# Softmax denominators of the second layer on ScalarE, and the low parts of its weights on GpSimd

## The chip, the cores and the metric

The kernel runs on one core of a Trainium2 chip, in one launch. The metric is the device time of that launch in microseconds (us). A core has TensorE (PE, matrix products; its weight loads are listed as PEld), VectorE (DVE), ScalarE (ACT), GpSimd (POOL) and SyncE (SP, which here issues all DMAs). Each engine takes its own instructions strictly in order; between engines there are only semaphores.

## The reference, cut to what matters

The program is one inference step of a two-layer encoder over 576 frames (512 of a prompt, 64 new ones with 256 cached). Layer 0 mixes with differential attention, layer 1 with forgetting attention (FoX); each is followed by a SwiGLU feed-forward part. The change lies in layer 1:

```python
def _fox_attend(q, k, v, cq, ck, q_pos, k_pos):
    s = jnp.einsum('bqhd,bkhd->bhqk', q, k) * (FOX_HEAD_DIM ** -0.5)
    s = s + cq^T[..., :, None] - ck^T[..., None, :]          # log-forget bias
    allowed = k_pos[None, :] <= q_pos[:, None]
    p = jax.nn.softmax(jnp.where(allowed, s, -jnp.inf), axis=-1)
    return jnp.einsum('bhqk,bkhd->bqhd', p.astype(v.dtype), v)
# 16 heads of 64; then  x += o @ w_o ;  x += swiglu(rmsnorm(x))
```

## The kernel before, in words

Activations lie transposed in SBUF, `xT` as 8 tiles of 128 features by 576 frames. Every weight comes as a stream of units of 128x1024 fp32, one unit for each 128 output columns. For precision each operand is split into a high and a low fp32r part: for a unit, ScalarE copies `w_raw` to `w_hi` (L908), and somebody subtracts `w_hi` from `w_raw` to give `w_lo`. TensorE adds the three products hi·hi, hi·lo and lo·hi (`slice_`, L570). There are two buffers of each, so unit u+1 is split while unit u is multiplied; the split of a unit must wait until the unit before the running one is used up (`w_used`).

`w_lo` is made by GpSimd (`lead`, L1262) in the feed-forward parts and in the output projections `wo`, and by VectorE (`weight_lo`, L1389) during both attention stages, where each unit has eight slots.

The attention of layer 1 is a schedule written out by hand. Time is cut into slots; a slot `t` holds one step of six matmuls of the projection (`project`). A group of two heads has 24 slots (three units: k, q, v). While group g+1 is projected, the attention of group g runs between the projection steps, and the last group runs between the steps of `wo`. The tables `F_...` name, for each small step and each engine, the slot `s` after the start of the group's attention in which it stands in that engine's queue. A slot orders an engine's own work; nothing else ties a step to a time.

For head h of group a the steps are: scores into `sps` (two banks; `score`, L635 to L643), row maximum on VectorE (L1462), exp on ScalarE (L1026), transposition on TensorE into `tps` (L658), its high part on ScalarE (`take_p`, L1048) and its low part on VectorE (`p_lo`, L1500), and the next transposition must wait for that low part, since `tps` is one buffer. Then come the products with V into `ops`: for the new frames (`pv_sample`, L694) and for the prompt (`pv_prompt`, L706). V is widened by ones, so the same product leaves the sum of each row, the softmax denominator, in the other 64 partitions of `ops`. VectorE takes its reciprocal into `rec` (L1516 for 64 new frames, L1526 for 512) and multiplies (L1518, L1528). The result is split for `wo` by ScalarE (`fox_o_hi`, L1065) and VectorE (`fox_o_lo`, L1534). `ops` and `tps` are free again only when `o_scaled` has been signalled by L1528; `transpose_v` of the next group (L671) and the next `pv_sample` wait for it.

Before the first group, GpSimd sets ones and zeros into the padded tiles of the layer and makes `f_lo`, the low part of the forget gate's weights (L1282), for which TensorE waits at L784.

Of the kernel before, what the change touches and what calls it, by code (L numbers as in the profile page):

```python
# [20 lines left out]
G = 8  # L21
# [19 lines left out]
WO_FOX_HI_AT, WO_FOX_SQ_AT = (50, 50, 52, 53, 53, 56, 58, 69), (52, 52, 52, 58, 60, 60, 62, 70)
WO_FOX_LO_AT, WO_FOX_SUM_AT = (51, 57, 57, 61, 62, 62, 64, 67), (50, 57, 57, 59, 62, 64, 67, 67)
WO_FOX_RES_AT = (7, 12, 19, 28, 35, 41, 47, 48, 50, 50, 52, 55, 58, 63)
WO_FOX_SPLIT_AT = (1, 10, 17, 24, 31, 45, 49, 55)
# [25 lines left out]
D_SPLIT = 1  # L70


F_SCORE, F_MAX, F_EXP = (2, 5, 5, 7, 7, 13, 13, 15, 18, 18), (1, 5, 5, 9, 10, 14, 14, 15, 18, 20), (1, 5, 6, 9, 9, 14, 14, 15, 18, 21)
F_TURN, F_TAKE_P, F_P_LO = (5, 7, 9, 11, 13, 15, 17, 18, 21, 24), (5, 7, 9, 11, 13, 15, 16, 18, 21, 23), (6, 7, 9, 11, 12, 15, 16, 18, 21, 22)
F_VT, F_TAKE_V, F_V_LO = (3, 2, 4)
F_PVS, F_TAKE_S, F_SUM_S = (7, 17), (8, 19), (9, 18)
F_PVP, F_SCALE_O, F_O_HI, F_O_LO = (15, 25), (15, 25), (16, 25), (17, 26)
F_K, F_Q, F_V = (8, 17, 24)
F_K_HI, F_K_LO, F_AUG = (11, 21), (13, 22), (17, 21)
F_Q_HI, F_Q_LO = (20, 21)  # L80
F_W_LO, F_SPLIT = (3, 1)
F_DUP_K, F_DUP_Q = (13, 23), 21
F_GATE_1, F_GATE_2, F_GATE_ACT = (9, 17, 13)
NORM0_AT = 3
NORM_AT = 2

# [52 lines left out]
def encoder(nc, w_units, w_forget, x_in, small, cst, cst16, rope_tab, k_past, v_past, f_past,  # L139
# [3 lines left out]
    with ExitStack() as ctx:  # L143
# [3 lines left out]
        def sem(name):  # L147
            return ctx.enter_context(nc.semaphore(name))
# [746 lines left out]
        def _(act):  # L895
# [244 lines left out]
            def fox_attention(t):  # L1140
                for a in range(G):
                    s, par, n = t - SLOTS * (a + 1), a % 2, Num(a)
                    for h in range(2):
                        if s == F_O_HI[h]:
                            fox_o_hi(a, h)
                    for tt in range(10):
                        if s == F_TAKE_P[tt]:
                            take_p(FOX, n, tt)
                    for jj in range(10):
                        if s == F_EXP[jj]:  # L1150
                            exps(FOX, n, par, jj)
# [102 lines left out]
        def _(pool):  # L1254
            def lead(u, kts=KT):

                u = u + 1
                slot = u.c % 2
                pool.wait_ge(w_hi_done, val(u + 1))
                if some(u - 1):  # L1260
                    pool.wait_ge(w_used, val(u - 1))
                nc.gpsimd.tensor_tensor(w_lo[slot][:, 0:kts, :], w_raw[slot][:, 0:kts, :],  # L1262
                                        w_hi[slot][:, 0:kts, :].bitcast(F32), ALU.subtract).then_inc(w_lo_done, 1)
# [5 lines left out]

            def fox_layer():  # L1270

                pool.wait_ge(w_used, U_LAYER)
                pool.wait_ge(acc_done, 3 * KT)
                for tile, value in ((vh2[:, :, 1:3, :], 1.0), (vl2[:, :, 1:3, :], 0.0)):
                    nc.gpsimd.memset(tile.bitcast(F32), value).then_inc(fox_set, 2)
                pool.wait_ge(fox_set, 4)
                nc.gpsimd.memset(kb[64:128, 0, :].bitcast(F32), 1.0).then_inc(fox_set, 1)
                pool.wait_ge(fox_set, 5)
                nc.gpsimd.memset(kb[0:64, 1, :].bitcast(F32), 1.0).then_inc(fox_set, 1)
                pool.wait_ge(fox_set, 6)  # L1280
                pool.wait_ge(f_hi_done, 1)
                nc.gpsimd.tensor_tensor(f_lo[:], f_raw[:], f_hi[:].bitcast(F32), ALU.subtract).then_inc(f_lo_done, 1)  # L1282
                nc.gpsimd.memset(kf[:, T:TQ], 0.0).then_inc(fox_set, 1)
                nc.gpsimd.memset(vf[:, T:TQ], 0.0).then_inc(fox_set, 1)
                for q in range(2):
                    nc.gpsimd.memset(qa[q][:, :, T:TQ].bitcast(F32), 0.0)
                    op = nc.gpsimd.memset(qb[q][:, :, T:TQ].bitcast(F32), 0.0)
                op.then_inc(fox_set, 1)
                for m in range(KT):
                    lead(Num(U_LAYER + U_WO + m))  # L1290

            pool.wait_ge(w_hi_done, 1)
            nc.gpsimd.tensor_tensor(w_lo[0][:, KT // 2:KT, :], w_raw[0][:, KT // 2:KT, :],
# [42 lines left out]
        def _(dve):  # L1336
# [165 lines left out]
            def o_sum(L, a, h):  # L1502

                dve.wait_ge(os_taken, val(v_index(L, a, h) + 1))
                if L == DIFF and later(a):
                    dve.wait_ge(ol_done, val(a))
                tt(og[:, SEQ:T] if L == DIFF else osum[:], os2[:, 0:NEW], os2[:, NEW:2 * NEW], ALU.add
                   ).then_inc(os_summed, 1)

            def scale_sample(a, h):  # L1510

                r, o, i = slice(64 * h, 64 * h + 64), slice(64 - 64 * h, 128 - 64 * h), 2 * a + h
                dve.wait_ge(os_summed, G + i + 1)
                if a > 0:
                    dve.wait_ge(op_lo, i - 1)
                nc.vector.reciprocal(rec[r, SEQ:T], osum[o, :]).then_inc(rec_done, 1)  # L1516
                dve.wait_ge(rec_done, 2 * i + 1)
                tt(rec[r, SEQ:T], osum[r, :], rec[r, SEQ:T], ALU.mult).then_inc(os_scaled, 1)  # L1518

            def scale_prompt(a, h):  # L1520

                r, o, i = slice(64 * h, 64 * h + 64), slice(64 - 64 * h, 128 - 64 * h), 2 * a + h
                dve.wait_ge(pvp_done, G + i + 1)
                if a > 0:
                    dve.wait_ge(op_lo, i - 1)
                nc.vector.reciprocal(rec[r, 0:SEQ], ops[o, :]).then_inc(rec_done, 1)  # L1526
                dve.wait_ge(rec_done, 2 * i + 2)
                tt(rec[r, 0:SEQ], ops[r, :], rec[r, 0:SEQ], ALU.mult).then_inc(o_scaled, 1)  # L1528

            def fox_o_lo(a, h):  # L1530

# [78 lines left out]
            def fox_attention(t):  # L1610
                for a in range(G):
                    s, par, n = t - SLOTS * (a + 1), a % 2, Num(a)
                    for h in range(2):
                        if s == F_SCALE_O[h]:
                            scale_prompt(a, h)
                        if s == F_O_LO[h]:
                            fox_o_lo(a, h)
                    for jj in range(10):
                        if s == F_MAX[jj]:
                            row_max(FOX, n, par, jj)  # L1620
                    if s == F_V_LO:
                        v_lo(FOX, n)
                    for tt_ in range(10):
                        if s == F_P_LO[tt_]:
                            p_lo(FOX, n, tt_)
                    for h in range(2):
                        if s == F_SUM_S[h]:
                            o_sum(FOX, n, h)
                            scale_sample(a, h)

            def fox_layer():
                dve.wait_ge(r_ready, 3)
                for t in range(SLOTS * G + WO_ALL):
# [242 lines left out]
```

## Time and profile before

| | us |
|---|---|
| median of 3 runs (1566.44 to 1574.3) | 1572.11 |
| the profiled execution, its own time | 1574.79 |
| its span, first to last instruction | 1572.8 |
| attention stage of layer 1, about | 790 to 1107 |

The profile shows busy time by engine, a timeline in 40 slices, the chain of work that ended last, groups of instructions by line, and for any stretch what each engine did, what it waited for and at what clock TensorE ran. A busy TensorE is not one at its peak: after idle stretches its granted clock can be at the lower of two levels.

### The profile page before, as it was taken

What the parts mean: (1) busy time and instruction counts of PE and PEld (TensorE: products, weight loads), DVE (VectorE), ACT (ScalarE), POOL (GpSimd) and SP (SyncE); (2) the same over time, 40 slices, a digit from 0 to 9 for tenths busy, and PEclk for the clock granted to TensorE, in tenths of its full rate; (3) what the DMA queues carried; (4) which work ended last, traced back from release to release, by engine and by line L of the source; (5) the groups of instructions that cost most, each with busy time, mean ns of one, the idle gap of its engine ahead of it and who ended that gap; (6) DMA issues with size and microseconds to landing.
All of it is one profiled execution on the core that took longest, in us unless ns stands there. A gap on an engine that the chain in (4) does not pass through costs nothing.

```text
span 1572.8 us, 28185 instructions
## 1 busy us (share of the span) xinstructions
PE 1492.7 (95%) x10911; PEld 1446.0 (92%) x10911; DVE 665.7 (42%) x1073; ACT 587.1 (37%) x988; POOL 433.9 (28%) x216
## 2 busy tenths in 40 slices
PE   6999999999999999998888888988999999999996
PEld 6899999999999999998888888888999999999996
DVE  6787786611111111221577777776611111111212
ACT  4566665432222222222344444443432222222121
POOL 2000002244444444334000000002344444443331
PEclk9999999999999999999999999989999999999998
DMA  5433332222222222223322222221222222222222
GB/s 170 126 99 109 102 99 81 67 81 80 80 81 84 88 80 75 84 87 104 88 73 79 80 82 82 82 71 49 68 81 83 88 82 80 80 80 85 84 78 83
DMA packets 47592, 135.04 MB, mean 86 GB/s; under 512 B 6480, under 2 KB 11088, under 8 KB 47520
## 3 DMA queue, kind: packets, MB, share of 16 engines
q1 hardware_dynamic: 47520, 134.06, 27.7%
q8 instruction: 48, 0.79, 0.2%
q14 instruction: 24, 0.20, 0.0%
HBM read 111.22 MB, written 11.83 MB: 78 GB/s over the span
## 4 chain that ended last, share of the span: by engine, by line
PE 87%; DVE 7%; issue 2%; ACT 2%; POOL 1%; DMA 0%; SPq 0%; DVEq 0%; ACTq 0%; POOLq 0%
PE ps L570 74%; DVE rec L1526 3%; PE ops L706 3%; PE tps L658 2%; PE sps L617 2%; PE ops L694 1%; PE sps L635 1%; PE sps L641 1%; DVE rec L1528 1%; PE tps L671 1%; PE sps L620 1%; PE sps L784 1%; PE ops L713 0%; DVE w_lo L1389 0%; PE sps L590 0%
## 5 line engine op out<-in xcount | busy, mean ns | idle before, releaser
L1262 POOL TENSOR_TENSOR w_lo<-w_raw,w_hi 128x1024 fp32r<-128x1024 f32 (+1 forms) x153 | 359.7, 2351 | 1108.5 <-ACT w_hi L908 1108.5
L570 PE MATMUL ps<-xh,w_hi 128*128 128x288 f32 x2176 | 487.0, 306 | 18.3 <-DVE xl L1729 11.5
L570 PE MATMUL ps<-xl,w_hi 128*128 128x288 f32 x2176 | 471.5, 299 | 0.0
L570 PE MATMUL ps<-xh,w_lo 128*128 128x288 f32 x2176 | 470.9, 298 | 0.0
L908 ACT ACTIVATE w_hi<-w_raw 128x1024 fp32r<-128x1024 f32 (+1 forms) x200 | 208.2, 1041 | 451.0 <-PE ps L570 448.4
L570 PEld LDWEIGHTS ps<-xh,w_hi 128*128 128x128 f32 x2176 | 354.2, 193 | 21.4 <-issue 20.1
L570 PEld LDWEIGHTS ps<-xl,w_hi 128*128 128x128 f32 x2176 | 356.3, 192 | 0.0
L570 PEld LDWEIGHTS ps<-xh,w_lo 128*128 128x128 f32 x2176 | 355.4, 191 | 0.0
L570 PE MATMUL ps<-hh,w_lo 128*128 128x288 f32 x704 | 150.8, 294 | 0.0
L570 PE MATMUL ps<-hh,w_hi 128*128 128x288 f32 x704 | 149.8, 294 | 0.0
L570 PE MATMUL ps<-hl,w_hi 128*128 128x288 f32 x704 | 149.5, 293 | 0.0
L1377 DVE TENSOR_TENSOR uf<-ps,rs 128x576 f32<-128x576 f32 x44 | 33.3, 757 | 231.7 <-PE ps L570 231.7
L1766 DVE TENSOR_TENSOR hl<-hf,hh 128x576 f32 (+1 forms) x44 | 33.4, 759 | 228.5 <-ACT hh L1229 228.5
L1371 DVE TENSOR_TENSOR xT<-ps,xT 128x576 f32<-128x576 f32 (+1 forms) x44 | 33.2, 755 | 224.0 <-PE ps L570 223.6
L570 PEld LDWEIGHTS ps<-hh,w_hi 128*128 128x128 f32 x704 | 113.3, 187 | 0.0
L570 PEld LDWEIGHTS ps<-hl,w_hi 128*128 128x128 f32 x704 | 112.5, 188 | 0.0
L570 PEld LDWEIGHTS ps<-hh,w_lo 128*128 128x128 f32 x704 | 112.4, 188 | 0.0
L1229 ACT ACTIVATE hh<-hf 128x576 f32 (+1 forms) x44 | 30.1, 685 | 178.3 <-POOL hf L1316 178.3
L1462 DVE TENSOR_REDUCE nmax<-sps 128x1 f32<-128x384 f32 (+3 forms) x160 | 74.8, 496 | 29.0 <-PE sps L620 20.4
L1500 DVE TENSOR_TENSOR ptl<-tps,pth 128x512 fp32r<-128x512 f32 (+1 forms) x96 | 46.8, 488 | 77.1 <-ACT pth L1048 77.0
L658 PE MATMUL tps<-cstf,pr 128*128 128x128 f32 x312 | 57.0, 285 | 20.9 <-DVE pts L1500 20.7
L1026 ACT ACTIVATE pr<-sps,nmax 128x384 f32<-128x384 f32 (+3 forms) x80 | 42.2, 538 | 59.1 <-DVE nmax L1462 58.6
(182 smaller groups left out, 1739.7 us busy)
## 6 DMA issues: line engine op xcount, KB each, us to landing
w_raw<-w_units SPq DMA_DIRECT2D x184, 512.0 KB, 3.5
w_raw<-w_units SPq DMA_DIRECT2D x16, 384.0 KB, 3.0
qsw<-qsin SPq DMA_DIRECT2D x64, 72.0 KB, 2.0
ka<-ka SPq DMA_DIRECT2D x16, 224.0 KB, 3.0
xT<-x_in SPq DMA_DIRECT2D x8, 288.0 KB, 5.5
dk_out<-kf SPq DMA_DIRECT2D x8, 288.0 KB, 2.5
dv_out<-vf SPq DMA_DIRECT2D x8, 288.0 KB, 2.2
fk_out<-kf SPq DMA_DIRECT2D x8, 288.0 KB, 2.2
```

Of the source, the lines that this page charges most:

```text
L570: mm = nc.tensor.matmul(out[:, half, :], w[:, k, :], rhs[:, kt, half * HALF:(half + 1) * HALF], start=start and w is w_hi[slot] and rhs is ...
L658: mm = nc.tensor.transpose(tps[:, b, :], pr[:, slot, P * b:P * b + P], ident)
L706: mm = nc.tensor.matmul(ops[:, P * j:SEQ], w, p[:, j, P * j:SEQ], start=j == 0 and v is hi and p is pth, stop=j == 3 and v is lo)
L908: nc.scalar.activation(w_hi[slot][:, 0:kts, :], w_raw[slot][:, 0:kts, :], ACT.Copy).then_inc(w_hi_done, 1)
L1026: nc.scalar.activation(pr[:, slot, 0:width(i)], sps[:, jj % 2, 0:width(i)], ACT.Exp, bias=nmax[:, slot:slot + 1]).then_inc(exp_done, 1)
L1262: nc.gpsimd.tensor_tensor(w_lo[slot][:, 0:kts, :], w_raw[slot][:, 0:kts, :], w_hi[slot][:, 0:kts, :].bitcast(F32), ALU.subtract).then_inc( ...
L1371: tt(halves(at(xT, k)), proj(n.c % 2), halves(at(xT, k)), ALU.add).then_inc(ps_read, 1)
L1377: tt(halves(dst), proj(n.c % 2), halves(scale), ALU.mult).then_inc(ps_read, 1)
L1462: nc.vector.tensor_reduce(nmax[:, slot:slot + 1], sps[:, jj % 2, 0:width(i)], AX_X, ALU.max, negate=True).then_inc(max_done, 1)
L1500: tt(dst, src, hi.bitcast(F32), ALU.subtract).then_inc(pt_lo, 1)
L1526: nc.vector.reciprocal(rec[r, 0:SEQ], ops[o, :]).then_inc(rec_done, 1)
L1766: tt(at(hl, jt), hf[:], at(hh, jt).bitcast(F32), ALU.subtract).then_inc(hl_done, 1)
```

## The change

- The two reciprocals of a head leave VectorE. ScalarE takes the logarithm of the new frames' denominators (`log_sample`, 64 columns) and of the prompt's (`recip`, 512 columns from `ops`), then one exp with factor -1 over all 576 columns. VectorE keeps the two multiplications (`scale_o`), now behind a wait for ScalarE.
- In layer 1's attention stage, `w_lo` of 23 units is made by GpSimd (`lead`) instead of VectorE (`weight_lo`).
- GpSimd makes `f_lo` first in the layer, ahead of its memsets.
- The slots of the layer's tables are shifted: `transpose_v` from 3 to 4, the first score from 2 to 3, the multiplication of head 0 from 15 to 16, high part of the output of head 0 from 16 to 17, and smaller ones.

```diff
-F_PVP, F_SCALE_O, F_O_HI, F_O_LO = (15, 25), (15, 25), (16, 25), (17, 26)
+F_PVP, F_SCALE_O, F_O_HI, F_O_LO = (15, 25), (16, 25), (17, 25), (17, 28)
+F_LN_S, F_RECIP = (10, 21), (15, 25)
-F_SCORE, ... = (2, 5, 5, 7, 7, 13, 13, 15, 18, 18), ...
+F_SCORE, ... = (3, 4, 5, 7, 7, 13, 13, 15, 18, 18), ...
-F_VT, F_TAKE_V, F_V_LO = (3, 2, 4)
+F_VT, F_TAKE_V, F_V_LO = (4, 1, 4)
@@ ScalarE
+            def log_sample(a, h):
+                r, o, i = slice(64 * h, 64 * h + 64), slice(64 - 64 * h, 128 - 64 * h), 2 * a + h
+                act.wait_ge(os_summed, G + i + 1)
+                if a > 0:
+                    act.wait_ge(op_lo, i - 1)
+                nc.scalar.activation(rec[r, SEQ:T], osum[o, :], ACT.Ln).then_inc(den_logs, 1)
+            def recip(a, h):
+                r, o, i = slice(64 * h, 64 * h + 64), slice(64 - 64 * h, 128 - 64 * h), 2 * a + h
+                act.wait_ge(pvp_done, G + i + 1)
+                nc.scalar.activation(rec[r, 0:SEQ], ops[o, :], ACT.Ln).then_inc(den_logs, 1)
+                act.wait_ge(den_logs, 2 * i + 2)
+                nc.scalar.activation(rec[r, :], rec[r, :], ACT.Exp, scale=-1.0).then_inc(rec_done, 1)
@@ GpSimd, fox_layer
+                pool.wait_ge(f_hi_done, 1)
+                nc.gpsimd.tensor_tensor(f_lo[:], f_raw[:], f_hi[:].bitcast(F32), ALU.subtract).then_inc(f_lo_done, 1)
                 pool.wait_ge(w_used, U_LAYER)
                 pool.wait_ge(acc_done, 3 * KT)
...
-                pool.wait_ge(f_hi_done, 1)
-                nc.gpsimd.tensor_tensor(f_lo[:], f_raw[:], f_hi[:].bitcast(F32), ALU.subtract).then_inc(f_lo_done, 1)
...
-                for m in range(KT):
-                    lead(Num(U_LAYER + U_WO + m))
+                for m in range(1, U_IN):
+                    lead(Num(U_LAYER + m))
@@ VectorE
-            def scale_sample(a, h):
...
-                nc.vector.reciprocal(rec[r, SEQ:T], osum[o, :]).then_inc(rec_done, 1)
...
-            def scale_prompt(a, h):
...
-                nc.vector.reciprocal(rec[r, 0:SEQ], ops[o, :]).then_inc(rec_done, 1)
...
+            def scale_o(a, h):
+                r, i = slice(64 * h, 64 * h + 64), 2 * a + h
+                dve.wait_ge(rec_done, i + 1)
+                tt(rec[r, 0:SEQ], ops[r, :], rec[r, 0:SEQ], ALU.mult).then_inc(o_scaled, 1)
                 tt(rec[r, SEQ:T], osum[r, :], rec[r, SEQ:T], ALU.mult).then_inc(os_scaled, 1)
@@ VectorE, fox_layer
-                    if t % KT == F_W_LO and KT <= t < SLOTS * G:
-                        weight_lo(U_LAYER + t // KT + 1)
```

## Rows read from the trace of the kernel before

**Rows 1.** The page: busy times, and the granted clock in 40 slices
```profile
PE 1492.7 (95%) x10911; PEld 1446.0 (92%) x10911; DVE 665.7 (42%) x1073; ACT 587.1 (37%) x988; POOL 433.9 (28%) x216
...
PEclk9999999999999999999999999989999999999998
```
**Rows 2.** Chain that ended last, 850 to 1180: by line, then start, us, what
```profile
by line: PE ps L570 43.7%; DVE rec L1526 13.3%; PE ops L706 7.9%; PE tps L658 4.9%; issue 4.3%; PE ops L694 3.1%; PE sps L635 2.8%; DVE rec L1528 2.7%; PE sps L641 2.5%; PE tps L671 1.8%; DVE nmax L1462 1.3%; DVE w_lo L1389 1.2%; ACT ka L97
...
954.48 1.58 PE ps L570 x12
```
**Rows 3.** Windows: stretch, length, busy us by engine, then PEclk, DMA share, GB/s
```profile
790.00:831.00 41.00, 36.21 (x246) 33.81 (x245) 30.84 (x46) 19.62 (x37) 0.00 (x0) 0.92 0.26 81
912.90:953.80 40.90, 35.59 (x243) 33.33 (x242) 30.61 (x46) 19.29 (x36) 0.00 (x0) 0.92 0.27 78
1070.00:1107.00 37.00, 33.38 (x239) 31.73 (x237) 21.47 (x33) 13.23 (x26) 7.38 (x3) 0.95 0.13 44
100.00:140.00 40.00, 40.00 (x300) 36.31 (x298) 31.42 (x72) 26.33 (x64) 0.00 (x0) 1.00 0.34 101
```
**Rows 4.** Timeline of TensorE, one group: idle time before, and its releaser
```profile
935.82 0.50 PE L706 MATMUL ops<-pth,vh 128*128 128x512 f32 x1 [0.57 <-DVE ptl L1500]
942.21 1.09 PE L671 MATMUL tps<-cstf,vf 128*128 128x128 f32 x4 [2.15 <-DVE rec L1528]
965.62 0.69 PE L658 MATMUL tps<-cstf,pr 128*128 128x128 f32 x4 [2.59 <-DVE pts L1500]
```
**Rows 5.** Timeline of VectorE in the same group
```profile
937.99 3.35 DVE L1526 RECIPROCAL rec<-ops 64x512 f32<-64x512 f32 x1 [0.31 <-PE ops L706]
941.37 0.69 DVE L1528 TENSOR_TENSOR rec<-ops,rec 64x512 f32<-64x512 f32 x1
...
964.67 0.54 DVE L1462 TENSOR_REDUCE nmax<-sps 128x1 f32<-128x384 f32 x1
965.14 0.34 DVE L1500 TENSOR_TENSOR pts<-tps,pts 128x192 fp32r<-128x192 f32 x1
```
**Rows 6.** Windows behind four idle times of TensorE, columns as in rows 3
```profile
745.40:751.40 6.00, 5.92 (x22) 5.36 (x23) 0.00 (x0) 0.75 (x2) 0.68 (x6) 0.53 0.01 3
775.30:779.30 4.00, 2.23 (x13) 1.79 (x13) 2.88 (x4) 3.57 (x5) 0.00 (x0) 1.00 0.62 122
...
942.20:946.20 4.00, 3.99 (x19) 3.91 (x19) 3.56 (x6) 2.29 (x5) 0.00 (x0) 0.58 0.04 9
...
1065.80:1069.80 4.00, 3.94 (x30) 3.55 (x31) 3.44 (x7) 2.45 (x7) 0.00 (x0) 1.00 0.01 4
```
**Rows 7.** ScalarE: groups of the whole span (busy, mean ns), then one window
```profile
L1079 ACT ACTIVATE ors<-ops,eps 128x512 f32<-128x512 f32 x8 | 5.5, 687 | 3.1 <-PE tps L714 3.1
L1083 ACT ACTIVATE ors<-ors 128x576 f32<-128x576 f32 x8 | 5.5, 686 | 0.3
...
L1225 ACT ACT_TABLE_LOAD x2 | 2.6, 1283 | 0.0
...
965.60:976.70 11.10, 10.52 (x70) 10.21 (x70) 7.56 (x15) 8.46 (x16) 0.00 (x0) 0.85 0.23 53
```
**Rows 8.** `w_lo` by VectorE; then GpSimd and VectorE at 718; L1348 over all
```profile
L1389 DVE TENSOR_TENSOR w_lo<-w_raw,w_hi x46: 1204/1216/1228, 31.0 to 1054.9; 128x1024 fp32r<-128x1024 f32 x46
...
718.21 2.40 POOL L1262 TENSOR_TENSOR w_lo<-w_raw,w_hi 128x1024 fp32r<-128x1024 f32 x1 [2.36 <-ACT w_hi L908]
...
718.97 2.26 DVE L1348 SCALAR_TENSOR_TENSOR xl<-xT,smalls,xh  x1 [1.08 <-ACT xh L922]
...
L1348 DVE SCALAR_TENSOR_TENSOR xl<-xT,smalls,xh x24: 805/814/2275, 297.5 to 1138.0; 128x576 fp32r<-128x576 f32 x16, - x8
```
**Rows 9.** Timelines of ScalarE, GpSimd and TensorE where the second layer begins
```profile
737.98 1.06 ACT L1160 ACTIVATE f_hi<-f_raw 128x1024 fp32r<-128x1024 f32 x1 [1.16 <-DMA f_raw<-w_forget]
...
742.99 2.34 POOL L1282 TENSOR_TENSOR f_lo<-f_raw,f_hi 128x1024 fp32r<-128x1024 f32 x1
...
745.48 0.82 PE L784 MATMUL sps<-xh,f_hi 128*128 128x288 f32 x2 [4.81 <-POOL f_lo L1282]
```

More of the change, by code:

```diff
@@ L40 @@
 WO_END = [max(q for q, s in enumerate(WO_STEPS) if s[0] == j) for j in range(WO_RUNS)]
[L41 to L44, printed above, removed]
+WO_FOX_HI_AT, WO_FOX_SQ_AT = (50, 50, 53, 53, 53, 55, 58, 69), (52, 52, 52, 57, 60, 60, 62, 70)
+WO_FOX_LO_AT, WO_FOX_SUM_AT = (51, 57, 57, 61, 62, 62, 64, 67), (50, 57, 57, 58, 62, 64, 67, 69)
+WO_FOX_RES_AT = (7, 12, 19, 29, 35, 47, 47, 48, 50, 50, 52, 57, 58, 63)
+WO_FOX_SPLIT_AT = (1, 12, 18, 24, 31, 45, 48, 55)
 WO_HI_AT, WO_SQ_AT = (49, 50, 51, 53, 53, 56, 58, 69), (50, 50, 54, 57, 60, 61, 61, 71)
@@ L70 @@
 D_SPLIT = 1
-F_SCORE, F_MAX, F_EXP = (2, 5, 5, 7, 7, 13, 13, 15, 18, 18), (1, 5, 5, 9, 10, 14, 14, 15, 18, 20), (1, 5, 6, 9, 9, 14, 14, 15, 18, 21)
+F_SCORE, F_MAX, F_EXP = (3, 4, 5, 7, 7, 13, 13, 15, 18, 18), (1, 5, 5, 9, 9, 12, 14, 15, 18, 18), (1, 5, 6, 9, 9, 14, 15, 15, 18, 19)
 F_TURN, F_TAKE_P, F_P_LO = (5, 7, 9, 11, 13, 15, 17, 18, 21, 24), (5, 7, 9, 11, 13, 15, 16, 18, 21, 23), (6, 7, 9, 11, 12, 15, 16, 18, 21, 22)
-F_VT, F_TAKE_V, F_V_LO = (3, 2, 4)
-F_PVS, F_TAKE_S, F_SUM_S = (7, 17), (8, 19), (9, 18)
-F_PVP, F_SCALE_O, F_O_HI, F_O_LO = (15, 25), (15, 25), (16, 25), (17, 26)
-F_K, F_Q, F_V = (8, 17, 24)
-F_K_HI, F_K_LO, F_AUG = (11, 21), (13, 22), (17, 21)
+F_VT, F_TAKE_V, F_V_LO = (4, 1, 4)
+F_PVS, F_TAKE_S, F_SUM_S = (7, 17), (8, 19), (7, 19)
+F_PVP, F_SCALE_O, F_O_HI, F_O_LO = (15, 25), (16, 25), (17, 25), (17, 28)
+F_LN_S, F_RECIP = (10, 21), (15, 25)
+F_K, F_Q, F_V = (9, 17, 24)
+F_K_HI, F_K_LO, F_AUG = (11, 21), (14, 22), (17, 21)
 F_Q_HI, F_Q_LO = (20, 21)
-F_W_LO, F_SPLIT = (3, 1)
-F_DUP_K, F_DUP_Q = (13, 23), 21
-F_GATE_1, F_GATE_2, F_GATE_ACT = (9, 17, 13)
+_, F_SPLIT = (3, 1)
+F_DUP_K, F_DUP_Q = (15, 23), 21
+F_GATE_1, F_GATE_2, F_GATE_ACT = (9, 19, 13)
 NORM0_AT = 3
@@ L352, in encoder @@
         fox_set = sem("fox_set")
+        den_logs = sem("den_logs")
         rec_done = sem("rec_done")
@@ L1143, in fox_attention @@
                     for h in range(2):
+                        if s == F_RECIP[h]:
+                            recip(a, h)
                         if s == F_O_HI[h]:
@@ L1156, in fox_attention @@
                             take_o_sample(FOX, n, h)
+                        if s == F_LN_S[h]:
+                            log_sample(a, h)
             def fox_layer():
@@ L1506, in o_sum @@
                     dve.wait_ge(ol_done, val(a))
+                if L == FOX and some(a * 2 + h):
+                    dve.wait_ge(os_scaled, val(a * 2 + h))
                 tt(og[:, SEQ:T] if L == DIFF else osum[:], os2[:, 0:NEW], os2[:, NEW:2 * NEW], ALU.add
                    ).then_inc(os_summed, 1)
-            def scale_sample(a, h):
[L1512 to L1515, printed above, removed]
-                nc.vector.reciprocal(rec[r, SEQ:T], osum[o, :]).then_inc(rec_done, 1)
-                dve.wait_ge(rec_done, 2 * i + 1)
-                tt(rec[r, SEQ:T], osum[r, :], rec[r, SEQ:T], ALU.mult).then_inc(os_scaled, 1)
-            def scale_prompt(a, h):
[L1522 to L1525, printed above, removed]
-                nc.vector.reciprocal(rec[r, 0:SEQ], ops[o, :]).then_inc(rec_done, 1)
-                dve.wait_ge(rec_done, 2 * i + 2)
-                tt(rec[r, 0:SEQ], ops[r, :], rec[r, 0:SEQ], ALU.mult).then_inc(o_scaled, 1)
+            def scale_o(a, h):
+                r, i = slice(64 * h, 64 * h + 64), 2 * a + h
+                dve.wait_ge(rec_done, i + 1)
+                tt(rec[r, 0:SEQ], ops[r, :], rec[r, 0:SEQ], ALU.mult).then_inc(o_scaled, 1)
+                tt(rec[r, SEQ:T], osum[r, :], rec[r, SEQ:T], ALU.mult).then_inc(os_scaled, 1)
             def fox_o_lo(a, h):
@@ L1614, in fox_attention @@
                         if s == F_SCALE_O[h]:
-                            scale_prompt(a, h)
+                            scale_o(a, h)
                         if s == F_O_LO[h]:
@@ L1628, in fox_attention @@
                             o_sum(FOX, n, h)
-                            scale_sample(a, h)
             def fox_layer():
```

## The prediction

> **What bounds the kernel now.** First the page: TensorE is busy for 95% of the span, at nearly its full clock but for one slice of 40 that shows an 8 [rows 1]. So most of the time belongs to TensorE and this change can't touch it. Then the chain of work that ended last, cut to the attention stage of the second layer: there the 512-column reciprocal L1526 alone holds 13.3% and its multiplication 2.7% [rows 2]. VectorE is on the path there, in front of TensorE.
>
> Then the stage group by group. One group of two heads takes 41 us, in which TensorE is busy for 36.2 in the first and 35.6 in a later one, at a granted clock of 0.92; the same stage of the first layer, which has no 512-column reciprocal, shows TensorE busy for 40.00 of 40 us at clock 1.00 [rows 3]. Between the two group rows shown lie two more groups, and behind them two, that read the same within 0.1 us. So a group loses two things: some 5.3 us of idle TensorE, and 0.08 × 41 = 3.3 us of speed.
>
> The timeline of TensorE names the idle times of one group: 2.15 us ahead of `transpose_v`, which waits for L1528; 2.59 us ahead of the transposition of head 1, which waits for `p_lo`; and 0.57 us ahead of the second `pv_prompt` [rows 4]. On VectorE the first is the reciprocal (3.35) and its multiplication (0.69) in a row, which `transpose_v` waits out; the second is the same pair for head 0, with a row maximum and the small `p_lo` queued behind it, done at 965.48, 0.14 us before TensorE starts [rows 5]. The clock: after the 2.15 us idle time the next 4 us are granted 0.58, between the two levels of 2.4 and 1.2 GHz; after 4.81 us, 0.53 over 6 us. After an equal 2.15 us at 1065.8 it stayed at 1.00, and so it did around the idle times of 775 to 779, 1.77 us in all [rows 6]. Short idle times keep the clock; long ones mostly lose it.
>
> **The change part by part.** *Reciprocals.* Out go 3.35 us and one of 64 columns for each head on VectorE; in come a logarithm of 512 columns, one of 64 and an exp of 576 on ScalarE. The first layer has a logarithm of 512 columns out of `ops` at 687 ns and an exp of 576 at 686 ns [rows 7]; the new ones have 64 partitions instead of 128, and I take the same time. So from the end of `pv_prompt` to `o_scaled`: 0.69 + 0.69 + 0.69 for the multiplication [rows 5] and some 0.2 for hand-overs, 2.3 us, against the 4.22 us that it takes now from 937.99 to 942.21 [rows 4, 5]. That alone brings 2.15 down to 0.25 us, and `transpose_v` stands one slot later, which is another 0.79 us of projection (12 matmuls, two slots, take 1.58 us [rows 2]). This idle time goes. At the second, `p_lo` no longer stands behind the reciprocal in VectorE's queue: it stands ahead of `scale_o`. But on ScalarE `take_p` now stands behind `recip`: ready 0.81 us after `pv_prompt`, it starts at about 1.4 us, and the exp of the next score follows it. I count 1.4 + 0.35 for `take_p`, 0.6 for that exp and 0.1 for the hand-over: 2.45 us, while TensorE has its own work until about 2.3 us. 2.59 us becomes 0.1 to 0.2. What is late next is the `pv_sample` of head 1, which waits for `scale_o`, at 2.9 us: 0.2 us more.
>
> *`w_lo` to GpSimd.* VectorE loses 23 instructions of 1.216 us, 28 us in all; GpSimd takes 2.40 us for one [rows 8]. A unit has eight slots, over 8 × 0.79 = 6.3 us, and TensorE needs `w_lo` only at the unit's first step, so the 1.2 us more lie under that. SP's next load waits for `w_lo` too, but stands five slots behind the split. The cover goes only if GpSimd starts over 2 us later than I assume. Per group VectorE falls from 30.6 us by 6.7 + 1.1 + 3.7 to about 19; ScalarE rises from 19.3 to 22.6 [rows 3, 5, 8]; GpSimd has 7.2. In a group of 32 to 34 us none is a bound by its sum.
>
> *What the move costs.* GpSimd's `w_lo` gets in VectorE's way. At 718.97 an `xl` of VectorE that normally takes 0.81 us took 2.26, begun while a `w_lo` of GpSimd ran from 718.21 to 720.61: it ended at 721.23, 0.6 us behind it [rows 8]. In the new queue ScalarE's split of a unit at slot 17 stands just ahead of head 0's `fox_o_hi` (0.68 us), so the `fox_o_lo` behind it meets a GpSimd instruction that has run for 0.6 us and waits out the other 1.8. Behind it on VectorE stand the row maxima of the last two scores and a `p_lo`; the exps, and TensorE's transposition of slot 21, wait for them. TensorE has 0.4 us of slack there; I count 1.0 us of idle time. The next stretch, up to the second `pv_prompt`, is full on ScalarE: 8.46 of 11.1 us busy, where TensorE by itself would need 11.1 - 0.6 - 0.15 × 11.1 = 8.9 [rows 7]. So the 0.57 us ahead of `pv_prompt` stays. Sum of new and remaining idle time: 0.1 + 0.2 + 1.0 + 0.6, some 2.0 us for each of seven groups (the eighth runs beside `wo` and has no such split). Bounds: 0, if the queues have more slack than I count, and 4, if every hand-over is late; I take 2.0, as the row at 718.97 is the same pair of engines.
>
> The Trainium skill (SBUF — State Buffer, "Who interferes with whom") says that a VectorE instruction with two inputs in SBUF and a GpSimd instruction that reads SBUF exclude each other, and that whichever begins second is blocked until the first ends. The row at 718.97 agrees. By that rule the sum is the one here; without it 1.5 us in each of seven groups, about 10 us, would come off.
>
> *Clock.* Idle times of 1 us or less should keep it at 1.00, as the 1.77 us around 775 do [rows 6]. Then the 3.3 us of each group come back.
>
> *`f_lo` first.* `f_hi` is done at 739.04, GpSimd starts `f_lo` at 742.99, and TensorE has waited 4.81 us when it starts at 745.48 [rows 9]. Made at once, `f_lo` is done at 741.4: 3.9 us sooner. The idle time left is about 0.9 us, so I count the 6 us at 0.53 back as well, 2.8 us [rows 6]. The memsets now end later, but are wanted only some 8 us on. The other shifted slots cost nothing that I can find: they order work that waits for TensorE anyway; if one does cost, it lies within the 0 to 4 us.
>
> **The sum.** Idle time to win: six groups from 790 to 1035.6 with 4.8 + 5 × 5.3 = 31.3, a seventh like them 4.8, the last stretch 3.6: 39.7. Speed: 7 × 3.3 + 0.05 × 37 = 25. Together 64.7 [rows 3]. Less 7 × 2.0 = 14: 50.7. With 3.9 + 2.8 at the start: 57.4. From the profiled execution's 1574.79 that gives 1517.4. The median shown is 2.7 us lower than that execution: 1515.
>
> **The rivals.**
> (a) *The new idle times don't appear.* For it speaks that in the first layer VectorE at 31.4 of 40 and ScalarE at 26.3 hold TensorE up nowhere [rows 3]; against it the row at 718.97. The 14 come back: 1501.
> (b) *The clock doesn't recover.* The remaining idle times cluster or grow to 2 us, and TensorE goes on losing speed behind them as it does now. For it speaks that ScalarE's stretch up to the second `pv_prompt` is nearly full and strictly in order [rows 7]; against it the idle times of 775. Then the 25 and the 2.8 stay lost: 1543.
> (c) *Logarithm and exp need different tables.* A table load takes 1283 ns [rows 7]; with two of them for each head the chain is 2.3 + 2.6 = 4.9 us, longer than 4.22, and `transpose_v` gains nothing: only `f_lo` remains, about 1566. That would be a change that doesn't do what it says. Against it: the first layer takes both functions in turn eight times, and the span's loads lie elsewhere [rows 7].
> The skill (ScalarE: Activation LUTs, "Table sets: the hidden batching unit") names one set that holds both; the trace agrees.
> (d) *Slower.* GpSimd's `w_lo` meets VectorE on TensorE's path three times in a group, for each unit and not only at slot 17. If each time TensorE stands for the 2.4 us and loses about 1.7 us of speed behind it (4 us at 0.58), a group pays 12.3 us and wins back 8.6: 3.7 × 7 = 26 more, less 6.7 at the start, 1591. It decides from 8.6 us of new idle time and lost speed in a group. Against it: at the other two splits VectorE mostly has instructions whose source is PSUM queued.
>
> **How the numbers follow.** Forecast 1515: 0.57, in its own bounds of 0 to 4 us a group 1501 to 1529. (a) 0.17, (b) 0.18, (c) 0.04, (d) 0.04. The range takes in (a) and (b): 1499 to 1544, and leaves out (c), (d) and the far ends. About 0.5%, 8 us, is what a measurement of this kernel can tell from no change: faster by more 0.93, within it 0.03, slower by more 0.04.
>
> **What would show it.** In the new profile: TensorE busy for all but about 2 us of a group, a group of 33 to 35 us, clock 0.98 or more between 790 and its end; no idle time over 0.5 us ahead of `transpose_v`; `fox_o_lo` of head 0 at over 2 us instead of 0.75, and an idle time of about 1 us behind it; the wait at L784 under 1.5 us. Wrong it is if `transpose_v` still waits, if the clock stays at 0.92, or if TensorE waits for GpSimd's `w_lo`.

## The result

| | median, us | ratio to before, 95% interval |
|---|---|---|
| before | 1572.41 (1566.44 to 1574.3, 4 runs) | |
| after | 1517.74 (1516.01 to 1519.7, 4 runs) | 0.9659 (0.963 to 0.9688) |

The forecast was 1515, in a range of 1499 to 1544. The profiled execution of after took 1518.45 us, with a span of 1516.7.

The page of after, its line of busy times and of the granted clock, against [rows 1]:

```profile
PE 1467.4 (97%) x10911; PEld 1422.0 (94%) x10911; DVE 588.8 (39%) x1018; ACT 609.9 (40%) x1036; POOL 491.5 (32%) x239
...
PEclk9999999999999999999999999999999999999998
```

VectorE is busy for 77 us less, ScalarE for 23 and GpSimd for 58 us more. Two slices of 40 showed an 8 before, the 27th and the last; the 27th, which lies in the stage, is back at 9. Now TensorE in one group of after; the columns are start, us, engine, line, operation, and the idle time before it with its releaser:

```profile
837.07 0.41 PE L660 MATMUL tps<-cstf,pr 128*128 128x128 f32 x2 [0.94 <-ACT pr L1028]
841.45 0.51 PE L708 MATMUL ops<-pth,vh 128*128 128x512 f32 x1 [0.68 <-DVE ptl L1522]
```

These are the only idle times of the group, and the same two stand in all seven, 34.1 us apart. Those of 2.15 and 2.59 us [rows 4] are gone; what remains is the 0.57 us ahead of the second `pv_prompt`, now 0.68, and a new one of 0.94 us. In place of the reciprocal stand a logarithm and an exp on ScalarE, then the multiplication on VectorE (ns of one, min/median/max, first and last start in us):

```profile
L1071 ACT ACTIVATE rec<-ops x16: 589/592/595, 794.2 to 1046.4; 64x512 f32<-64x512 f32 x16
L1073 ACT ACTIVATE rec<-rec x16: 681/686/687, 794.8 to 1047.0; 64x576 f32<-64x576 f32 x16
L1538 DVE TENSOR_TENSOR rec<-ops,rec x16: 670/683/695, 796.2 to 1047.7; 64x512 f32<-64x512 f32 x16
```

Two windows of after answer to [rows 3] and [rows 6] (stretch, length, busy us of PE, PEld, DVE, ACT and POOL, PEclk, DMA share, GB/s):

```profile
815.70:849.80 34.10, 32.48 (x243) 30.27 (x242) 20.96 (x39) 22.09 (x43) 7.47 (x3) 1.00 0.33 94
773.00:777.00 4.00, 1.92 (x7) 1.48 (x8) 3.13 (x4) 1.78 (x4) 2.16 (x1) 0.77 0.89 221
```

A group is 34.1 us long instead of 40.9, TensorE is idle in it for 1.6 us instead of 5.3, and its clock is 1.00 instead of 0.92. The second window is the one bad spot of the new stage: its beginning. There VectorE and GpSimd of after read:

```profile
763.20 0.61 DVE L1690 TENSOR_SCALAR ncum<-cumh 32x896 f32<-32x896 f32 x1 [1.02 <-ACT cumh L1214]
763.84 1.08 DVE L1693 TENSOR_TENSOR ncum<-cumh,cum 32x896 f32<-32x896 f32 x1
764.95 2.71 DVE L1690 TENSOR_SCALAR ncum<-cumh 32x896 f32<-32x896 f32 x1
```
```profile
764.18 2.99 POOL L1284 TENSOR_TENSOR w_lo<-w_raw,w_hi 128x1024 fp32r<-128x1024 f32 x1 [14.48 <-ACT w_hi L910]
```

The same instruction takes 0.61 us alone and 2.71 beside GpSimd's `w_lo`, which runs until 767.17. It negates the cumulative forget sums, on the chain to the first score, and so TensorE waits longer there:

```profile
741.84 0.51 PE L786 MATMUL sps<-xh,f_hi 128*128 128x288 f32 x2 [0.96 <-POOL f_lo L1295]
...
773.83 0.42 PE L637 MATMUL sps<-ka,qa 128*128 128x384 f32 x1 [3.92 <-issue]
775.50 0.69 PE L643 MATMUL sps<-kb,qb 128*128 128x384 f32 x1 [1.25 <-DMA qb<-qa]
```

The first row is the wait for `f_lo`, 0.96 us instead of 4.81 [rows 9]. The second and third are the first score: 5.2 us of idle time. (What the profile calls "issue" ends 0.1 us after VectorE's `fox_q_lo`, for which that score waits.)

Three marks in TensorE's timeline split the difference: the end of the layer's first unit (the start at L786 less its idle time), the first product of the first `pv_prompt`, and the first product of the last block of the last one. The distances between them, in us, read in the same way from one profiled execution of each kernel below:

| | first unit to first `pv_prompt` | from there to the last | from there to the end of the span |
|---|---|---|---|
| before | 54.7 | 304.7 | 472.7 |
| after | 51.3 | 253.7 | 470.8 |
| only the reciprocals moved | 47.7 | 247.0 | 471.1 |
| only `w_lo` moved | 59.7 | 304.8 | 472.4 |
| only `f_lo` first | 48.3 | 305.4 | 472.7 |
| after, `fox_o_hi` of head 0 at 16 | 51.9 | 256.6 | 470.5 |
| after, late `aug_left` and `fox_q_lo` | 52.3 | 262.1 | 470.9 |
| after, early split | 47.7 | 253.9 | 471.2 |
| these three together | 49.0 | 264.9 | 472.2 |
| after, memsets for `w_lo` | 49.4 | 242.9 | 470.5 |
| after, `fox_o_hi` and `fox_o_lo` at 16 | 52.0 | 241.9 | 471.5 |
| the same with the early split | 50.4 | 241.8 | 471.1 |
| only the reciprocals moved, old slots | 50.1 | 251.2 | 471.5 |

So after gains 3.4 us at the start, 51.0 in the attention stage and 1.9 behind it. The first column is the least sure: kernels with the same instructions at the start of the layer differ in it by up to 2.7 us, by the clock that the execution got there: the early split alone reads 47.7 and together with both `fox_o` edits 50.4, with 5.1 us of idle time each, but with a granted clock of 1.00 over 775 to 779 in the one and 0.50 over 771.5 to 775.5, the like place, in the other.

### The profile page after: what moved, and what is told of

It reads as the page before. It is cut to its first block, busy times and chain, and to the rows that moved or that the text cites. A ratio compares the mean times of both kernels' runs of the same rounds, so it can differ in the third digit from the quotient of the medians.

```text
span 1516.7 us, 28200 instructions
## 1 busy us (share of the span) xinstructions
PE 1467.4 (97%) x10911; PEld 1422.0 (94%) x10911; DVE 588.8 (39%) x1018; ACT 609.9 (40%) x1036; POOL 491.5 (32%) x239
## 4 chain that ended last, share of the span: by engine, by line
PE 90%; ACT 3%; DVE 3%; issue 2%; DMA 1%; POOL 0%; SPq 0%; DVEq 0%; ACTq 0%
PE ps L572 78%; PE ops L708 3%; PE tps L660 2%; PE sps L619 2%; PE sps L637 1%; PE sps L643 1%; PE ops L696 1%; ACT w_hi L910 1%; DVE ol L1545 1%; PE sps L622 1%; PE tps L673 0%; PE ops L715 0%; DMA xT<-x_in 0%; PE sps L786 0%; ACT ka L976 0%
## 5 line engine op out<-in xcount | busy, mean ns | idle before, releaser
L1284 POOL TENSOR_TENSOR w_lo<-w_raw,w_hi 128x1024 fp32r<-128x1024 f32 (+1 forms) x176 | 417.3, 2371 | 995.6 <-ACT w_hi L910 995.6
L572 PE MATMUL ps<-xh,w_hi 128*128 128x288 f32 x2176 | 481.6, 303 | 16.4 <-ACT xh L1223 8.7
L572 PEld LDWEIGHTS ps<-xh,w_hi 128*128 128x128 f32 x2176 | 349.6, 190 | 19.4 <-issue 17.9
L572 PEld LDWEIGHTS ps<-xh,w_lo 128*128 128x128 f32 x2176 | 351.8, 189 | 0.0
L572 PEld LDWEIGHTS ps<-xl,w_hi 128*128 128x128 f32 x2176 | 351.8, 189 | 0.0
L1393 DVE TENSOR_TENSOR xT<-ps,xT 128x576 f32<-128x576 f32 (+1 forms) x44 | 33.2, 755 | 224.6 <-PE ps L572 224.3
L1338 POOL TENSOR_TENSOR hf<-sg,uf 128x576 f32<-128x576 f32 x44 | 62.8, 1427 | 0.0
```

The lines of the kernel that those rows point to most:

```text
L572: mm = nc.tensor.matmul(out[:, half, :], w[:, k, :], rhs[:, kt, half * HALF:(half + 1) * HALF], start=start and w is w_hi[slot] and rhs is ...
L1338: nc.gpsimd.tensor_tensor(hf[:], sg[:], uf[:], ALU.mult).then_inc(hf_done, 1)
L1393: tt(halves(at(xT, k)), proj(n.c % 2), halves(at(xT, k)), ALU.add).then_inc(ps_read, 1)
```

## The experiments

My theory behind them: TensorE was held up by VectorE's queue behind the reciprocal, and the idle time cost its length and the clock after it; the move of `w_lo` brings nothing of that and costs, because GpSimd shuts VectorE out. The rival: VectorE was simply too full, and both loads had to leave it.

**Only the reciprocals moved.** In the changed kernel, back to `w_lo` on VectorE:

```diff
 # VectorE, fox_layer
+                    if t % KT == F_W_LO and KT <= t < SLOTS * G:     # F_W_LO = 3
+                        weight_lo(U_LAYER + t // KT + 1)
 # GpSimd, fox_layer
-                for m in range(1, U_IN):
-                    lead(Num(U_LAYER + m))
+                for m in range(KT):
+                    lead(Num(U_LAYER + U_WO + m))
```

> The changed kernel, with w_lo of the attention stage's 23 units made by VectorE again (at slots 3, 11 and 19, as before the change). My theory (VectorE's queue behind the reciprocal held TensorE up; the move of w_lo is no part of the gain and costs the 0.94 us idle time behind fox_o_lo in each of 7 groups): 1518 us +-8, no fox_o_lo over 1 us, group between 33 and 35 us, but a new idle time of about 1 us where v_lo stands behind w_lo on VectorE. Rival (VectorE's total load was the bound, so that both reciprocals and w_lo have to leave it): a group over 36 us, 1535 or more.

Measured: 1505.71 us, ratio 0.9593 (0.9575 to 0.9612): faster than after, the intervals don't overlap, and it lies below the 1518 ± 8 that I expected. Here is one of its groups, then what remains of idle time in it:

```profile
810.20:843.40 33.20, 32.59 (x243) 30.42 (x242) 22.76 (x41) 22.12 (x42) 0.00 (x0) 1.00 0.33 97
```
```profile
865.93 0.50 PE L708 MATMUL ops<-pth,vh 128*128 128x512 f32 x1 [0.28 <-DVE ptl L1522]
873.68 0.55 PE L660 MATMUL tps<-cstf,pr 128*128 128x128 f32 x3 [0.34 <-DVE vl L1512]
```

The idle time behind `v_lo` is there, at 0.34 us a third of what I expected. VectorE with 22.8 of 33.2 us busy holds TensorE up for no more than these 0.6 us. The rival falls: the reciprocals, with `f_lo` and the new slots, are more than the whole gain, and moving `w_lo` costs 10 to 12 us of it (10 by the two ratios, 12 by the two medians).

**Only `w_lo` moved.** In the kernel before:

```diff
-                    if t % KT == F_W_LO and KT <= t < SLOTS * G:
-                        weight_lo(U_LAYER + t // KT + 1)
 # GpSimd, fox_layer
-                for m in range(KT):
-                    lead(Num(U_LAYER + U_WO + m))
+                for m in range(1, U_IN):
+                    lead(Num(U_LAYER + m))
```

> The kernel before, with only w_lo of the attention stage moved to GpSimd; reciprocals, slots and f_lo as before. My theory: both idle times of 2.1 and 2.6 us behind the reciprocals stay, a group takes 40 to 41.5 us, 1572 +-6 us. Rival (VectorE's total load was the bound): half of the gain or more, 1550 or less.

Measured: 1577.17 us, ratio 1.0048 (1.0029 to 1.0067): a small loss. The groups are as long as before (304.8 us to the last `pv_prompt`, 304.7 before), and both idle times of TensorE stand as they did [rows 4]:

```profile
864.61 0.63 PE L671 MATMUL tps<-cstf,vf 128*128 128x128 f32 x4 [2.15 <-DVE rec L1528]
887.16 1.09 PE L658 MATMUL tps<-cstf,pr 128*128 128x128 f32 x4 [2.59 <-DVE pts L1500]
```
```profile
846.39:887.16 40.77, 35.75 (x242) 33.33 (x242) 30.56 (x42) 19.26 (x37) 7.44 (x3) 0.92 0.27 79
849.41 2.69 DVE L1534 TENSOR_TENSOR ol<-rec,oh 64x576 fp32r<-64x576 f32 x1
```

But VectorE is not freer: it loses 3.7 us of `w_lo` in a group, and reads busy for 30.56 us in the window, as before [rows 3]. GpSimd shuts out `fox_o_lo` here too, 2.69 us instead of 0.75, and `osum`, 1.56 instead of 0.22, in 7 groups. So the run shows that this move by itself shortens neither idle time; what a VectorE really freed of 3.7 us would do, it doesn't show. The loss lies at the start of the layer, 59.7 against 54.7 us. There `ncum` takes 2.70 us, as in after.

**Only `f_lo` first.** In the kernel before, the two lines of `f_lo` ahead of `pool.wait_ge(w_used, U_LAYER)`:

> The kernel before, with only f_lo moved ahead of GpSimd's memsets. My theory: the wait at L784 falls from 4.8 to about 1 us and the clock behind it stays at 1.00, and nothing later in the start of the layer takes that back: 6 us less, 1566. Rival (the chain from the forget gate to the first score takes it back): 2 us less or nothing, 1570 to 1572.

Measured: 1565.99 us, ratio 0.9973 (0.9961 to 0.9986), 4.2 us less (2.2 to 6.1). The wait at L784 is 1.05 us, and the first `pv_prompt` comes 6.4 us sooner after the first unit (48.3 instead of 54.7); the next stretch is 0.7 us longer in the profile. The size at that place is as forecast, what comes out at the end of it is a little less.

**GpSimd writing but not reading.** In the changed kernel, for the 23 units of the attention stage:

```diff
-                lead(Num(U_LAYER + m))         # tensor_tensor w_lo <- w_raw, w_hi
+                nc.gpsimd.memset(w_lo[u % 2][:].bitcast(F32), 0.0).then_inc(zeroed, 1)
+                pool.wait_ge(zeroed, m)
+                nc.gpsimd.memset(w_lo[u % 2][:].bitcast(F32), 0.0).then_inc(w_lo_done, 1)
```

> The changed kernel, with GpSimd's subtraction for w_lo of the attention stage's 23 units replaced by two memsets of the same tile one after the other, so that GpSimd writes and doesn't read; it leaves out the low part of those weights. My theory (reading is what shuts out a VectorE instruction with two inputs in SBUF): fox_o_lo of head 0 takes 0.75 us although GpSimd runs beside it, the idle time behind it goes, about 1511. Rival (any GpSimd instruction shuts VectorE out): fox_o_lo still lasts until GpSimd's memset ends, over 1.2 us.

Measured: 1503.29 us in one run. VectorE's `fox_o_lo` in it, and GpSimd beside it:

```profile
860.38 0.75 DVE L1554 TENSOR_TENSOR ol<-rec,oh 64x576 fp32r<-64x576 f32 x1 [0.16 <-ACT oh L1084]
```
```profile
859.84 0.95 POOL L1317 MEMSET w_lo<- 128x1024 f32 x1 [10.53 <-ACT w_hi L911]
860.85 0.96 POOL L1319 MEMSET w_lo<- 128x1024 f32 x1
```

GpSimd runs, and `fox_o_lo` takes its 0.75 us, beginning 0.54 us into a memset. In after it reads

```profile
833.45 2.48 DVE L1545 TENSOR_TENSOR ol<-rec,oh 64x576 fp32r<-64x576 f32 x1 [0.16 <-ACT oh L1083]
```
```profile
832.93 2.39 POOL L1284 TENSOR_TENSOR w_lo<-w_raw,w_hi 128x1024 fp32r<-128x1024 f32 x1 [10.09 <-ACT w_hi L910]
```

and ends at 835.93, 0.6 us after GpSimd. So for this instruction it is GpSimd's reading that shuts VectorE out. The Trainium skill (SBUF — State Buffer, "Who interferes with whom") says just this of a VectorE instruction with two inputs in SBUF, and that a GpSimd instruction that only writes does not exclude it; both rows agree. The time lies 8 us below the 1511 expected: the 0.94 us are gone in all groups, the 0.68 us ahead of `pv_prompt` are down to 0.26, and `ncum` at the start of the layer keeps its time.

**Who begins first.** Two kernels on one question: can order alone save `fox_o_lo`? In the changed kernel:

```diff
 # first
-F_O_HI, F_O_LO = (17, 25), (17, 28)
+F_O_HI, F_O_LO = (16, 25), (17, 28)
 # second
-F_O_HI, F_O_LO = (17, 25), (17, 28)
+F_O_HI, F_O_LO = (16, 25), (16, 28)
```

> The changed kernel, with fox_o_hi of head 0 at slot 16 instead of 17, so that it stands on ScalarE ahead of the split of a weight unit, and fox_o_lo on VectorE begins before GpSimd's w_lo. My theory (VectorE's fox_o_lo is shut out while GpSimd reads): fox_o_lo 0.75 instead of 2.47 us, the 0.94 us idle time behind it goes in 7 groups, 6 us less than the changed kernel: 1511. Rival (the idle time comes from ScalarE's order and not from fox_o_lo's length): 1517 to 1518, the idle time at slot 21 stays.

Measured: 1519.47 us, ratio 0.9682 (0.9666 to 0.9698): no gain. `fox_o_hi` stands ahead of the split now, but the eviction of q stands ahead of `fox_o_lo` on VectorE:

```profile
830.60 0.75 DVE L1399 TENSOR_TENSOR qf<-ps,rs 128x576 f32<-128x576 f32 x1
831.26 2.74 DVE L1545 TENSOR_TENSOR ol<-rec,oh 64x576 fp32r<-64x576 f32 x1
```
```profile
830.99 2.41 POOL L1284 TENSOR_TENSOR w_lo<-w_raw,w_hi 128x1024 fp32r<-128x1024 f32 x1 [10.48 <-ACT w_hi L910]
```

GpSimd begins 0.27 us before it, and the idle time behind is longer (1.33 us). My edit had not done what I meant it to do. The second does:

> The changed kernel, with both fox_o_hi and fox_o_lo of head 0 at slot 16, so that fox_o_lo stands on VectorE ahead of the q projection's eviction too and begins before GpSimd's w_lo does. My theory (of fox_o_lo and w_lo the one that begins second waits, and with only fox_o_hi moved fox_o_lo still began 0.27 us too late): fox_o_lo at 0.75 us in all 8 groups, no idle time at slot 21, GpSimd's w_lo later instead without anyone waiting for it; 6 us less than the changed kernel, about 1511. Rival (the idle time at slot 21 has another cause in the order of the queues): it stays near 1 us, 1517 to 1520.

Measured: 1505.38 us, ratio 0.9582 (0.9562 to 0.9602), 12 us less than after. A window as long as one group, which is now 32.4 us, and VectorE against GpSimd:

```profile
797.80:830.20 32.40, 32.40 (x243) 30.39 (x242) 19.31 (x39) 22.12 (x43) 7.48 (x4) 1.00 0.35 99
```
```profile
828.71 0.75 DVE L1545 TENSOR_TENSOR ol<-rec,oh 64x576 fp32r<-64x576 f32 x1 [0.75 <-ACT oh L1083]
```
```profile
830.19 2.40 POOL L1284 TENSOR_TENSOR w_lo<-w_raw,w_hi 128x1024 fp32r<-128x1024 f32 x1 [10.48 <-ACT w_hi L910]
```

TensorE is busy without a break, and `fox_o_lo` is over before GpSimd begins. The gain is twice what I had expected for this run: I had counted the 0.94 us alone, but the 0.67 us ahead of the second `pv_prompt` goes with it. The two were for the most part one delay, handed on through ScalarE's queue. In after, the row maximum stands behind `fox_o_lo`, and the exp behind the row maximum:

```profile
835.86 0.60 DVE L1484 TENSOR_REDUCE nmax<-sps 128x1 f32<-128x256 f32 x2
```
```profile
836.30 0.73 ACT L1028 ACTIVATE pr<-sps,nmax 128x256 f32<-128x256 f32 x2 [1.57 <-DVE nmax L1484]
```

From there ScalarE works without a listed break up to the copy (`take_p`) for which VectorE's last `p_lo`, and so the second `pv_prompt`, waits. With the memsets, where `fox_o_lo` is short at its old slot, 0.26 of the 0.68 us stays; that part goes only with the new order.

**The idle time ahead of `pv_prompt`, by later steps.**

```diff
-F_AUG = (17, 21)         # aug_left, ScalarE
+F_AUG = (17, 23)
-                        if s == F_Q_LO:                       # 21
+                        if s == (F_Q_LO if g else 21):        # 23
```

> The changed kernel, with aug_left of head 1 (0.78 us on ScalarE) and fox_q_lo (1.52 us on VectorE, group 0 left as it was) moved behind the last transposition's take_p and p_lo, from slot 21 to 23. My theory (the 0.67 us ahead of the second pv_prompt is ScalarE's and VectorE's queue ahead of that last p_lo): the idle time falls under 0.2 us in 7 groups, 4 us less than the changed kernel, 1514. Rival (it is the plain latency of transposition, copy and subtraction): it stays at 0.5 us or more, 1517 to 1518.

Measured: 1525.46 us, ratio 0.9706 (0.9688 to 0.9724): 8 us more than after. The idle time there does fall below what a listing shows, but `fox_q_lo` has moved into the next `w_lo`:

```profile
877.67 3.62 DVE L1475 SCALAR_TENSOR_TENSOR qa<-qf,qa 64x576 fp32r<-64x576 f32 x2
```
```profile
878.02 2.65 POOL L1284 TENSOR_TENSOR w_lo<-w_raw,w_hi 128x1024 fp32r<-128x1024 f32 x1 [6.92 <-ACT w_hi L910]
```

Two instructions of 0.76 us take 3.62; the multiplication behind them starts 2 us late, and TensorE stands for 1.06 us ahead of the first score of the next group. The same mechanism again, in a place that I had not looked at.

**The early split.** ScalarE splits the layer's fourth unit before it waits for the cumulative sums, so that `w_lo` is over before `ncum`:

```diff
 # ScalarE, forget
+                lead(Num(U_LAYER + 2))
                 act.wait_ge(f_step, 8)
                 nc.scalar.activation(cumh[:], cum[:], ACT.Copy).then_inc(cum_hi, 1)
```

(and the slot loop leaves that unit out).

> The changed kernel, with ScalarE's split of the fourth weight unit of the layer moved ahead of its wait for the cumulative sums, so that GpSimd's w_lo of that unit is over before VectorE negates the sums (ncum). My theory (that ncum instruction took 2.71 instead of 0.61 us because GpSimd was reading and writing beside it, and it lies on the chain to the first score): ncum back to 0.61 us, first score 2 us sooner, clock behind it better kept: 3 us less than the changed kernel, 1515. Rival (the chain to the first score is bounded elsewhere, by the copies by DMA): 1517 to 1518.

Measured: 1515.3 us, ratio 0.9643 (0.9626 to 0.9661). From the first unit to the first `pv_prompt` it is 47.7 us instead of 51.3; the wait of the first score falls from 3.92 to 2.06 us, and `ncum` is short again:

```profile
765.02 0.62 DVE L1691 TENSOR_SCALAR ncum<-cumh 32x896 f32<-32x896 f32 x1
```
```profile
771.82 0.41 PE L637 MATMUL sps<-ka,qa 128*128 128x384 f32 x1 [2.06 <-issue]
```

The place is right: with the early split (or the memsets) the first column of the table reads 47.7 to 50.4 us, in the kernels of after without it 51.3 to 52.4. The 2.4 us of the whole time are near the 3 expected, though its two intervals overlap.

**Together.** The first edit of `fox_o_hi`, the late steps and the early split:

> The edits of the three runs with fox_o_hi at slot 16, the late aug_left and fox_q_lo, and the early split, together in the changed kernel. My theory (they are separate idle times of TensorE): the sum of the three, 13 us less, 1505, and a group of 32.5 us without idle time over 0.3 us. Rival (each idle time taken out shows up in the next wait): 1511 or more.

Measured: 1526.11 us, ratio 0.9714 (0.9694 to 0.9734). Of the three only the early split helped by itself, and the sum shows it: 49.0 us at the start, 264.9 in the attention stage. The run was planned as a sum of gains of which two were none.

Then the edit that puts both `fox_o_hi` and `fox_o_lo` at slot 16, with the early split and without the late steps:

> The same edit together with the early split of the fourth weight unit. My theory: the two idle times are separate, 6 + 3 us less than the changed kernel, about 1508; that is still not below the kernel in which only the reciprocals moved (1505.7), since the idle time ahead of the second pv_prompt remains. Rival (w_lo on GpSimd can be made free by order alone): 1505 or less.

Measured: 1502.66 us, ratio 0.9576 (0.9557 to 0.9594): both edits that work, in the changed kernel. It is the fastest of the full kernels tried here, below before and after; from the kernel with only the reciprocals moved it can't be told apart. It lies 2.7 us below the `fox_o_lo` edit alone, the size that the early split had by itself, but these two intervals overlap as well. I had expected 1508, with the 0.67 us ahead of `pv_prompt` still in it.

**The slots.** The kernel with only the reciprocals moved, with the layer's tables `F_SCORE` to `F_GATE` as they were before the change (those of `wo` stay as in after):

> The kernel in which only the reciprocals moved (w_lo on VectorE, f_lo first), but with the slots of the layer as they were before the change, the multiplication of head 0 at slot 15 again. My theory (the reciprocals are the gain, the slots trim it): about 0.3 us ahead of transpose_v, and 1.0 us ahead of the transposition of head 1, because the small p_lo stands behind the multiplication and its wait for ScalarE; 1515. Rival (without new slots the waits stay long): 1.5 us or more at both places with a clock of 0.95 or less, 1530 or more.

Measured: 1512.44 us, ratio 0.9629 (0.961 to 0.9648). A group takes 33.7 us (the two idle times below are that far apart), and the one idle time that comes back is

```profile
861.10 0.63 PE L660 MATMUL tps<-cstf,pr 128*128 128x128 f32 x4 [0.68 <-DVE pts L1522]
894.79 0.63 PE L660 MATMUL tps<-cstf,pr 128*128 128x128 f32 x4 [0.68 <-DVE pts L1522]
```

at the transposition of head 1, 0.68 instead of the 1.0 expected; ahead of `transpose_v` there is none. So the new slots are worth some 6 us where `w_lo` stays on VectorE (5.7 by the ratios, 6.7 by the medians, though the intervals still touch); the other 57 are the reciprocals, `f_lo` and the tables of `wo`.

## Why the prediction was right, point by point

- **VectorE's reciprocal held TensorE up.** Right, and shown: with the reciprocals on ScalarE both idle times are gone, with the old slots too but for 0.68 us; with `w_lo` alone moved both stay. The new chain took what was counted: the logarithm 0.59 us (0.69 counted), the exp 0.69, the multiplication 0.68. The 13.3% of L1526 [rows 2] were read as a share of the stage; that stretch runs 73 us past its end, and over 790 to 1107 the share is 17.0%.
- **The clock comes back.** Right: 1.00 in every group. That the idle times and the clock are two parts of one loss is read from the windows; no run changed the clock alone. Idle times per group fell by 5.3 - 1.6 = 3.7 us, a group by 6.8, so close to half of the gain is speed. One reading was wrong and cost nothing: the page before shows two slices with an 8, not one [rows 1].
- **2.0 us of idle time per group remain.** Measured 1.6. Two of the four small terms, 0.1 us ahead of head 1's transposition and 0.2 ahead of its `pv_sample`, did not show as idle times; 1.0 was 0.94 and 0.6 was 0.67.
- **GpSimd shuts out `fox_o_lo`.** Right in place, in size (2.48 us; "over 2" was said), and in what it costs: the prediction gave some 10 us for the stage without it, and the run with the order turned round gave 11.8 (253.7 to 241.9). It took both idle times off there, 1.5 us a group, which my later expectation for that run forgot.
- **`f_lo` first.** Counted at 6.7; 6.4 at its place in the one profiled execution, and 4.2 (2.2 to 6.1) at the end when made alone.
- **What failed: the start of the layer.** The prediction's sum there was 6.7 us, and after gained 3.4. The step that was missing is `ncum` on VectorE, which GpSimd's `w_lo` of the fourth unit shuts out for 2.1 us on the chain to the first score. The prediction said that `w_lo` on GpSimd lies under cover at every unit but looked for the collision only at slot 17. That the whole time came out so near is in part luck. From one profiled execution to the other the gain is 56.3 us where 57.4 were counted: 3.3 too few at the start, 0.3 more in the stage (51.0 for 50.7, with idle time down by more than counted and speed up by less), and 1.9 behind the stage's last `pv_prompt`. Of these 1.9, 1.0 is a wait of 1.02 us in `wo`, at 1107.12 before, which no listing of after shows; the rest is not traced to a cause.
- **What was said without being asked.** "The other shifted slots cost nothing": they bring some 6 us, where it was measured. And the price of moving `w_lo` was put into the sum as 10 us, without the conclusion that this half of the change is a loss as it stands: it costs 10 to 12 us against the kernel that leaves it out, and nothing that can be measured once the order is turned.
- **The rivals.** (a) and (b) did not come, nor (c): the logarithm and the exp follow each other without a load between them. (d) had a true mechanism at the wrong scale: in after it hits one instruction of a group, `fox_o_lo` of head 0, not three.

## What to carry to other kernels

Look for what a slow instruction has queued behind it on its in-order engine, not for how full the engine is: the kernel that left `w_lo` on VectorE, 22.8 of 33.2 us busy, was the faster one, and taking a reciprocal of 3.35 us out of the way of two steps of TensorE brought the stage. When work goes to GpSimd, list every VectorE instruction that can run beside it and reads SBUF twice (`ncum`, which reads it once, was hit too), and place those that TensorE waits for so that they begin first. Idle times that follow each other through an in-order queue may be one delay: take away the first, and count again before adding gains.

## What the runs showed of the hardware that I had not expected

A VectorE instruction with only one input in SBUF can be shut out too: the negation `ncum` (tensor_scalar, 32x896, SBUF to SBUF) took 2.71 us instead of 0.61 beside GpSimd's subtraction. Beside a memset of GpSimd it kept its time, and the memset paid:

```profile
762.73 0.64 DVE L1699 TENSOR_SCALAR ncum<-cumh 32x896 f32<-32x896 f32 x1
```
```profile
761.95 0.95 POOL L1317 MEMSET w_lo<- 128x1024 f32 x1 [14.90 <-ACT w_hi L911]
762.96 1.32 POOL L1319 MEMSET w_lo<- 128x1024 f32 x1
```

The second memset, begun inside `ncum`, takes 1.32 us instead of 0.95. So beside this kind of instruction writing alone can be enough to collide. That order alone decides is not shown for it: `ncum` itself began 0.17 us before the first memset's recorded end and took 0.64 us, hardly more than its 0.61.

GpSimd waits too where it begins second: in after its `w_lo` at 764.18 began inside VectorE's subtraction of 763.84 to 764.92, which reads two tiles of SBUF, and took 2.99 us, where another one took 2.39.

TensorE kept its full clock through an idle time of 1.33 us in each group (the run with `fox_o_hi` at 16, window behind it):

```profile
835.15:839.15 4.00, 3.71 (x27) 3.48 (x27) 2.16 (x4) 3.89 (x9) 0.00 (x0) 1.00 0.38 88
```

while 2.15 us cost it at 942.2 and not at 1065.8 [rows 6].
